# A fourth group in seven products, two more in the last layer, and queries taken out earlier in the second half of a two-layer trunk

## What is computed

```python
for l in range(DEPTH):                                   # DEPTH = 2
    h = _rmsnorm(x, norm_gain[l])
    proj = jnp.einsum('bsd,de->bse', h, w_in[l])         # 2048 -> 4352
    q, k, v, g_attn, x_rnn, g_rnn = jnp.split(proj, splits, axis=-1)
    attn = _swa_sink_attention(q, k, v, sinks[l], cos, sin)
    xc = _causal_conv(x_rnn, conv_w[l], conv_b[l])
    rnn = _rg_lru(xc, w_rgate[l], b_rgate[l], w_igate[l], b_igate[l], lru_param[l])
    mixed = jnp.concatenate([attn * jax.nn.silu(g_attn), rnn * jax.nn.silu(g_rnn)], axis=-1)
    x = x + jnp.einsum('bse,ed->bsd', mixed, w_out[l])   # 2048 -> 2048
return _rmsnorm(x, final_gain)
```

## Time and profile before

| | us |
|---|---|
| median of 3 runs | 2293.84 |
| lowest, highest | 2290.21, 2299.67 |
| the profiled execution: its own time | 2285.01 |
| its span in the trace | 2283.2 |
| PE busy | 2275.7 (100%) |
| DVE busy | 1568.7 (69%) |
| ACT busy | 1315.0 (58%) |
| POOL busy | 84.9 (4%) |

### The profile page before, as it was taken

How to read it: one execution, slowest core, us unless ns; L and a number is a source line. 1 busy time by engine, 2 the same in 40 slices (tenths; PEclk the granted TensorE clock), 3 DMA queues, 4 the chain that set the end, 5 groups by cost and what they waited for, 6 DMA issues and landing times.

```text
span 2283.2 us, 38210 instructions
## 1 busy us (share of the span) xinstructions
PE 2275.7 (100%) x14446; PEld 1939.6 (85%) x14446; DVE 1568.7 (69%) x2594; ACT 1315.0 (58%) x2536; POOL 84.9 (4%) x138
## 2 busy tenths in 40 slices
PE   9999999999999999999999999999999999999998
PEld 7888888899888888889988888888988888888898
DVE  7658778656546876856677777785568468778555
ACT  7558666444455867645565575663446557566444
POOL 1110000000111000000011100000000000000000
PEclk9999999999999999999999999999999999999999
DMA  8987777544788777644479866654545346666444
GB/s 255 258 234 259 238 241 239 156 135 142 212 245 233 252 235 240 214 142 138 139 233 267 263 206 203 214 190 146 141 130 170 99 134 196 208 202 196 140 134 153
DMA packets 173271, 447.01 MB, mean 196 GB/s; under 512 B 20768, under 2 KB 25120, under 8 KB 167200
## 3 DMA queue, kind: packets, MB, share of 16 engines
q1 hardware_dynamic: 165744, 381.56, 52.4%
q0 software_dynamic: 6912, 62.92, 11.4%
q10 hardware_dynamic: 432, 0.10, 0.0%
HBM read 365.85 MB, written 141.56 MB: 222 GB/s over the span
## 4 chain that ended last, share of the span: by engine, by line
PE 98%; DMA 1%; DVE 0%; ACT 0%; issue 0%; POOL 0%; ACTq 0%; DVEq 0%; POOLq 0%
PE proj L719 74%; PE proj L740 18%; PE ps_at L848 2%; PE ps_at L823 1%; PE ps_at L867 1%; PE proj L759 1%; DMA wall<-in_w 1%; PE proj L786 0%; ACT wcut L942 0%; PE ps_at L674 0%; DVE acc L1439 0%; ACT operand L979 0%; PE ps_at L801 0%; ACT sqr L1005 0%; DVE operand L1416 0%
## 5 line engine op out<-in xcount | busy, mean ns | idle before, releaser
L719 PE MATMUL proj<-operand,wcut 128*128 128x512 f32 x7512 | 1745.2, 391 | 0.3 <-DVE operand L1416 0.3
L719 PEld LDWEIGHTS proj<-operand,wcut 128*128 128x128 f32 x7512 | 1400.0, 188 | 297.4 <-issue 9.6
L1344 DVE TENSOR_TENSOR wcut<-wall,wcut 128x512 fp32r<-128x512 f32 x799 | 550.1, 688 | 537.1 <-ACT wcut L942 530.5
L942 ACT ACTIVATE wcut<-wall 128x512 fp32r<-128x512 f32 x798 | 501.9, 629 | 596.9 <-DMA wall<-in_w 322.8
L740 PEld LDWEIGHTS proj<-operand,wcut 128*128 128x128 f32 x1476 | 187.8, 191 | 6.5
L740 PE MATMUL proj<-operand,wcut 128*128 128x256 f32 x1476 | 189.8, 283 | 0.0
L740 PE MATMUL proj<-xsum_out,wcut 128*128 128x256 f32 x1104 | 136.8, 283 | 0.0
L740 PEld LDWEIGHTS proj<-xsum_out,wcut 128*128 128x128 f32 x1104 | 134.9, 192 | 0.6
L740 PE MATMUL proj<-xsum_in,wcut 128*128 128x256 f32 x864 | 111.8, 284 | 0.0
L740 PEld LDWEIGHTS proj<-xsum_in,wcut 128*128 128x128 f32 x864 | 107.9, 191 | 3.5 <-issue 1.7
L1048 ACT ACTIVATE gy<-proj 32x512 f32<-32x512 f32 x144 | 85.0, 590 | 14.9 <-PE proj L719 9.5
(11 more groups left out here) (186 smaller groups left out, 1733.6 us busy)
## 6 DMA issues: line engine op xcount, KB each, us to landing
wall<-in_w SPq DMA_DIRECT2D x494, 256.0 KB, 2.8
weight_cuts<-wcut SPq DMA_DIRECT2D x126, 512.0 KB, 3.9
wcut<-weight_cuts SPq DMA_DIRECT2D x126, 512.0 KB, 4.2
weight_sums<-in_blocks POOLq DMA_DIRECT2D x84, 512.0 KB, 6.6
wall<-weight_sums SPq DMA_DIRECT2D x164, 256.0 KB, 2.7
wall<-in_blocks SPq DMA_DIRECT2D x141, 256.0 KB, 2.8
weight_sums<-weight_sums POOLq DMA_DIRECT2D x28, 512.0 KB, 5.0
x<-in_xt SPq DMA_DIRECT2D x16, 512.0 KB, 3.7
```

Source lines behind the costliest of these rows:

```text
L719: last = pe.matmul(bank_of(l, 2 * g + m)[:, :], wcut[:, n % RING, a, c:c + P], operand[:, k, b, :], start=(i == 0 and k == 0), stop=(k == ...
L942: act.activation(wcut[:, u % RING, 0, :], wall[:, u % RING, 1, :], ACT.Copy).then_inc(w_hi, 1)
L1344: dve.tensor_tensor(wcut[:, u % RING, 1, :], wall[:, u % RING, 1, :], wcut[:, u % RING, 0, :].bitcast(F32), ALU.subtract).then_inc(w_lo, 1)
```

## The change

Half 1 gets group 16 in seven products in both layers, and groups 5 and 6 in the last layer. Group 16's split tiles join the stored ones. Those of groups 5 and 6 don't: a new constant `FIRST` = 7 keeps them out, so they are split on the chip in half 1. In half 0 the built groups run as *block* units, with as many matmuls as plain ones but another order of reading the operand. In half 1 the query tiles are taken out at slots 16, 17, 24, 25, 32, 33, 40, 41. POOL's additions open in six stretches instead of three, and there are 17 batches instead of 16, all of two groups. The reload of `x` moves from slot 127 to 135 with `IN_LAST`. In `rope` the wait for the shift stands ahead of the first multiplication instead of behind it.

```diff
-IN_LAST = 15
-IN_SEVEN = {(0, 0): (), (0, 1): (), (1, 0): range(7, IN_LAST + 1), (1, 1): range(7, IN_LAST + 1)}
+FIRST = 7
+IN_LAST = 16
+IN_SEVEN = {(0, 0): (), (0, 1): (), (1, 0): range(7, IN_LAST + 1), (1, 1): range(5, IN_LAST + 1)}
...
-    if h == 0 and zone_of(g) == "in" and g in BUILT[l] and (kind, j) != ("block", WHOLE[A21]):
+    if h == 0 and FIRST <= g < PG and g in BUILT[l] and (kind, j) != ("block", WHOLE[A21]):
...
-Q_AT = [2 * UPG + 4 * t for t in range(AT)]
+Q_AT = [[2 * UPG + UPG * (t // 2) + (4, 1)[h] * (t % 2) for t in range(AT)] for h in range(HALVES)]
...
-OPENS = {5: (0, 1, 1), 11: (1, 0, 4)}
+OPENS = {5: (0, 0, 128), 6: (0, 1, 1), 12: (0, 1, 130), 13: (1, 0, 138), 14: (1, 1, 12)}
...
             def rope(h, l, n, tile):
 
+                dve.wait_ge(shift_done, per_layer(h, l, 4 * (AT + 1), 4 * n + 4))
                 dve.tensor_tensor(gy[:, 0, :], bank_of(l, tile)[:, :], tab[:, 0, :], ALU.mult)
-
-                dve.wait_ge(shift_done, per_layer(h, l, 4 * (AT + 1), 4 * n + 4))
```

More of the change, by code:

```diff
@@ L1247, in _ @@
                             key_cross(h, l)
-                        if s in Q_AT:
-                            t = Q_AT.index(s)
+                        if s in Q_AT[h]:
+                            t = Q_AT[h].index(s)
                             shift(h, l, t + 1, tile_of("q", t))
@@ L1781, in _ @@
                         for t in range(AT):
-                            if s == Q_AT[t] + 1:
+                            if s == Q_AT[h][t] + 1:
                                 query(h, l, t)
```

## The result

The changed kernel takes 2319.79 us (median of 6, 2316.51 to 2321.39) against 2289.97 for the kernel before (median of 6, 2288.08 to 2299.67): ratio 1.0126, 95% interval 1.0113 to 1.0139. Forecast were 2311.8 us and a range of 2294 to 2320. So the sign and the range held, the range by 0.2 us; two of the six times lie over it. The time is nearest to rival (c), *more is late*, at 2321, which had a chance of 0.06.

A forecast was written before the change was run, and what follows sets the result against it. PE, almost always busy, bounds the kernel. Terms -3.3 + 2.5 + 2.35 + 0.65 + 5.8 + 6.9 + 2.1 + 1.0 = +18.0 us on the profiled 2285.0 give 2303.0, a median of 2311.8; range 2294 to 2320.

The forecast's parts named there:

- rival (c): Additions late beside fully split groups 5 and 6, clock falling also at the 3.9 us wait: +27, 2321 us; chance 0.06.
- What bounds the kernel: PE busy 2275.7 of 2283.2 us: fewer matmuls gain one for one, reordering on ACT or DVE can't gain.
- The matmuls: Four groups in seven products: 192 matmuls of 512 columns go, 336 of 256 come, gaining 3.3 us.
- The counted waits: PE waits from packed queries: slots 16-22 of (1, 1) 2.5, (1, 0) 2.35, 0.65 and 5.8, bank 6.9 us.
- the bank: (1, 1), slot 44: group 6's first lead unit waits for query tiles 6 and 7's bank, 6.9 us.
- the 0.7 at slot 22 of (1, 1): PE waits for slot 22's low part, behind the values' turn and tile 1 on DVE: 0.7 us.
- the 1.9: (1, 0): slot 45's low part, behind tile 7's shift and the other four exponents, 1.9 us late.
- Rival (a): Waits absorbed in part, mainly the bank wait of 6.9 staying: about +6.5, 2300 us; chance 0.27.
- Half 0, group 16: `mixed_hi` waits for slot 131's end, slot 134's low part 0.5 us late: 1.0 us over two passes, bounds 0 and 4.
- The clock: One drop to half rate, at the 6.9 us wait, costing 2.1 us, bounds 0 and 4.
- The additions at nothing, bound 3: POOL's six stretches: emptying (1, 0) returns nothing, weights in last layer's slots 13 to 40 may come late; 0, bound 3.
- The step from the profile to the median: Median of before lay 8.8 us above its profile, so 2303.0 became a median of 2311.8 us.

The follow-up runs named there:

- 4: Kernel before with only the openings of POOL's additions moved to the changed kernel's kind of stretches: 2287.8 us, ratio 0.998.
- 12: The kernel of 4 measured once more, unchanged: 2287.6 us, ratio 0.9986.
- 1: Kernel before with only half 1's query tiles taken out at the changed kernel's slots (16, 17, 24, 25, ...): 2306.8 us, ratio 1.0066.
- 2: Changed kernel with the old spacing of query tiles (16, 20, 24, ...) in (1, 0) alone: 2309.8 us, ratio 1.0072.
- 8: Changed kernel with query tiles four slots apart again, except tiles 5 and 7 at slots 33 and 42 of (1, 1): 2307.7 us, ratio 1.0075.
- 9: The kernel of 8 with additions moved: batch 5 to slot 150 of (0, 0), last five batches from slot 4 of (1, 0): 2300.4 us, ratio 1.0049.
- 5: The kernel of 4 with group 16 of both layers in seven products, groups 5 and 6 plain, queries as before: 2291.4 us, ratio 1.0007.
- 6: The kernel of 5 with batch 5 of the additions opened at slot 150 of (0, 0) instead of 128: 2290.2 us, ratio 0.9996.
- 3: Changed kernel with additions' batch 5 from slot 150 of (0, 0) and batch 11 from slot 130 of (0, 1): 2315.9 us, ratio 1.0102.
- 10: The kernel of 9 with its last five batches spread: two in (1, 0) from slot 4, one from 138, two in (1, 1): 2295.8 us, ratio 1.0019.
- 7: Changed kernel without group 6 in seven products in (1, 1), packed queries kept: 2313.4 us, ratio 1.0096.

## Why the forecast came out as it did

**What bounds the kernel: right.** PE had no slack, its waits came out in the time, some of them with slow matmuls on top, and nothing that was moved on ACT or DVE gained. Transfers are another matter: the prediction had it that nothing comes back from the emptied stretch, and moving the additions alone gave 3.4 us (4 and 12).

**The matmuls: right**, 192 whole ones fewer and 336 halves more.

**The counted waits: right within 0.7 us at all eight places.** Forecast against the trace: slots 21, 22 and 30 of (1, 0) 0.95, 1.4, 0.65 against 1.1, 1.0, 0.9; slots 44 to 46 there 1.9 and 3.9 against 1.8 and 3.5; slot 21 of (1, 1) 1.85 against 1.9; the bank 6.9 against 7.5, with the chain as told, each step within 0.6 us. Only the 0.7 at slot 22 of (1, 1) didn't come. Sum: 18.25 counted, 17.8 seen. One wait ended for another reason than told: the 1.9 was to be slot 45's low part behind the four exponents, and PE stood already in slot 44, for the exponents themselves (L824 <- ACT `prob`), one step earlier in the same chain. Experiments 1, 2, 8 and 9 take these waits away or bring them alone. Rival (a), that they would be absorbed, fell. But the argument against it, that the chain has no transfer in it, holds for the changed kernel only: in experiment 1 two waits for transfers stood in that chain and the count was 3.2 us short at slot 44 (5.1 for 1.9).

**Half 0, group 16: half right.** 0.7 us per pass in slot 134 for 0.5. The term missed what the same held-up ACT meets next: 2.2 us in slot 140 of (0, 0), within its bound of 4, due to batch 5 of the additions beside it (5 and 6).

**The clock: mis-sized.** One fall for 2.1 us was counted, three came for 5.9 us. The step that failed was to look for it only at the longest wait, because the clock had held for 4.3 us behind PE's last matmul; inside the kernel it fell behind waits of 2.5 and 3.5 us too. The latter was set aside for rival (c), and the third place wasn't known to wait at all. The cost of one, 2.1 us, was about right: 1.5, 1.6 and 2.8.

**The additions at nothing, bound 3: wrong.** This is the step that failed most. I looked at the stretch that was emptied and at where its load went in the last layer, and took "PE stood at no transfer at 0.90" for a bound. I didn't count what each stretch holds. From slot 1 of (0, 1) ran five full batches and one of a single group; now, with group 16 and the batch of groups 5 and 6, six full ones. Their last addition starts 17 us later, 11 of it later against PE, beside the stores of the tiles, and ACT waits 13.4 us for weights. It cost 5.6 us of waits at slots 58 to 66 of (0, 1), 1.6 of clock and the 2.2 above: 9.4 us. Experiments 3, 6, 9 and 10 take them away, 3 and 6 by moving batches alone; in 7, with one batch of the stretch half as large, those of (0, 1) are gone as well. Rival (c) had the additions late too, but beside groups 5 and 6 in (1, 1), and they were late in half 0.

**The step from the profile to the median: wrong, and it hid the rest.** I carried over that the median of before lay 8.8 us above its profile. After's lies 1.3 under its own. Against its own trace, 2303.0 forecast and 2321.1 seen, the sum was 18 us short; 9.4 are the additions with their fall, 2.8 + 1.5 - 2.1 = 2.2 more of the clock, and 2.9 are two waits of 1.4 at slots 52 and 53 of (0, 0), which come and go from run to run: 8 has neither, and up to that place its program is that of the changed kernel. The other 3.6 us are in waits too short to name, or were not found. The offset of 8.8 gave half of it back. That the forecast landed no more than 8 us from the median, and that the range held by 0.2, was luck.

## What to carry to other kernels

A chain that goes ACT, DVE, ACT, DVE can be counted from the rows of before to within 0.7 us at the eight places here, even where none of its steps waits yet, as long as no transfer comes late into it (experiment 1); it is worth doing at each place where two uses of a shared bank or buffer are brought nearer. What such a count of one chain doesn't give is two covered delays that meet: late weights and a held-up ACT each cost nothing alone in (0, 0) and 3 us of waiting together. So when work is added to a background queue, follow its end as well as its start, and look at what else changed beside the place where it now ends.

## What the runs showed of the hardware

The granted clock fell behind short waits of PE. Behind those of 4.4 us (experiment 3), 3.5 and 2.5 (the changed kernel), 3.1 (7), 3.0 (5) and 2.8 (2) it was at 0.50, which is 1.2 GHz, for a while, and behind single ones of 2.2 us, at slot 140 of (0, 0) and 58 of (0, 1) in the changed kernel, it stayed at 1.00. Two in a row were enough, though: in experiment 3 PE waited 1.8 and 2.0 us at slots 44 and 46 of (1, 0), and the window from 1288 to 1302 has a clock of 0.76. The Trainium skill ("TensorE: Matmul & The Clock Gate", section "HAM oscillation — how this bites in real kernels") describes a kernel that pays for its waits on TensorE twice, once idle and once in matmuls at half rate behind them. These traces agree: behind the six waits above the second payment was 1.6 to 2.8 us, half to four fifths of the wait itself, and in (1, 1), where half of the slow time fell within the wait of 7.5 us, it was 1.5, a fifth of it.

A DMA share near full hurt or didn't by where it lay. In experiment 5 it was 1.02 in the window where PE waited, with the clock down right behind:

```profile
423.00:428.00 5.00, 2.20 (x7) 1.66 (x7) 2.31 (x3) 3.36 (x5) 0.52 (x1) 0.87 1.02 396
```

At 0.92 in (1, 0) before, PE was busy all of the 20 us. So the share alone tells no wait. Nor does the sum of ACT's waits for weights: it was 18.0 us in experiment 4 and 13.7 in 5. What grew with PE's wait in the windows compared here was the longest of them, 6.0 in 5 against 3.9 in 4, and 7.7 after against 4.0 before in (0, 1). Elsewhere before had one of 8.9 us and PE waited for nothing, so where it falls counts as well.
